# Expert retrieval of a streaming encoder layer: routing of a tile begins in the last third of the tile in front of its own, and selection is dealt out over 29 fours instead of 21

## The reference, cut to what matters

```python
q = (xb @ w_query).reshape(PEER_BLOCK, PEER_HEADS, 2, D_HALF)      # 8 heads, 2 halves, 128
s = einsum('thpd,hpkd->thpk', q, sub_keys)                         # 128 keys a half
sv, si = lax.top_k(s, 16)                                          # 16 lists of scores
cand = sv[:, :, 0, :, None] + sv[:, :, 1, None, :]                 # 256 sums a head
fv, fi = lax.top_k(cand.reshape(..., 256), 16)
eidx = take_along_axis(cidx, fi);  g = softmax(fv)
a = einsum('thkd,td->thk', expert_u[eidx], xb)
w = g * gelu(a)
out = einsum('thk,thkd->td', w, expert_v[eidx])
```

## Time and profile before

| | before |
|---|---|
| median of 3 runs | 3683.89 us (3681.74 to 3687.78) |
| the profiled execution's own time | 3686.14 us |
| its span, first to last instruction | 3684.3 us |
| busy TensorE, VectorE, ScalarE, GpSimd | 86%, 63%, 20%, 30% of the span |
| granted TensorE clock, mean over the span | 0.985 |
| bytes read from HBM | 1260.12 MB |

### The profile page before, as it was taken

How to read it: one execution, slowest core, us unless ns; L and a number is a source line. 1 busy time by engine, 2 the same in 40 slices (tenths; PEclk the granted TensorE clock), 3 DMA queues, 4 the chain that set the end, 5 groups by cost and what they waited for, 6 DMA issues and landing times.

```text
span 3684.3 us, 48012 instructions
## 1 busy us (share of the span) xinstructions
PE 3158.2 (86%) x17895; PEld 1389.9 (38%) x17895; DVE 2311.1 (63%) x6107; ACT 719.1 (20%) x2373; POOL 1110.6 (30%) x1177
## 2 busy tenths in 40 slices
PE   6999999889888878988887898889788888977776
PEld 3545556634334324423432343344234334422222
DVE  1333343867757866775776677677667757765444
ACT  2434434311111111111111111111111111111111
POOL 0000000033333333333333333333333333333332
PEclk8999999799999999999999999999999999999999
DMA  5000114299999999999999999999999999999997
GB/s 217 24 29 23 35 34 169 91 401 421 421 421 419 418 414 417 413 414 420 415 414 420 416 414 415 417 418 416 412 417 416 416 416 418 413 414 420 419 418 326
DMA packets 192682, 1275.60 MB, mean 346 GB/s; under 512 B 21056, under 2 KB 24768, under 8 KB 44608
## 3 DMA queue, kind: packets, MB, share of 16 engines
q0 software_dynamic: 165888, 1208.03, 79.4%
q1 hardware_dynamic: 26560, 64.49, 4.9%
HBM read 1260.12 MB, written 12.32 MB: 345 GB/s over the span
## 4 chain that ended last, share of the span: by engine, by line
DMA 46%; PE 35%; DVE 9%; issue 5%; POOL 4%; ACT 1%; SPq 0%; DVEq 0%; POOLq 0%; ACTq 0%
DMA arena<-in_experts,arena 45%; PE PS L1353 10%; PE PS L1182 8%; PE PS L1367 7%; POOL arena L651 4%; DVE arena L976 4%; PE PS L1276 3%; PE PS L1166 2%; PE PS L1399 2%; PE PS L1265 1%; PE PS L1225 1%; DVE arena L1051 1%; DVE arena L1054 1%; DVE arena L1057 1%; PE PS L1205 0%
## 5 line engine op out<-in xcount | busy, mean ns | idle before, releaser
L1353 PE MATMUL PS<-arena 128*128 128x512 bf16 x6912 | 1655.6, 382 | 453.1 <-DVE arena L976 440.6
L976 DVE CUSTOM_DVE_ANT_0 arena<-arena,PS 128x1024 f32<-128x1024 f32 x1152 | 1396.2, 1221 | 871.7 <-DMA arena<-in_experts,arena 548.4
L651 POOL DMA_INDIRECT arena<-in_experts,arena x1152 | 1089.0, 945 | 1938.0 <-PE PS L1367 1572.7
L1353 PEld LDWEIGHTS PS<-arena 128*128 128x128 bf16 x6912 | 611.5, 98 | 1480.5 <-DVE arena L976 865.1
L1367 PE MATMUL PS<-arena 128*32 128x512 f32 x4608 | 558.8, 603 | 16.8 <-ACT arena L867 16.8
L861 ACT ACTIVATE arena<-arena 128x4 f32<-128x4 f32 x288 | 59.5, 207 | 2156.2 <-DVE arena L976 2137.0
L1182 PE MATMUL PS<-arena 128*128 128x512 f32 (+1 forms) x720 | 309.8, 567 | 13.9 <-DMA arena<-in_w_in 7.9
L1399 PEld LDWEIGHTS PS<-arena 128*128 128x128 f32 x2304 | 266.6, 192 | 101.5 <-issue 101.5
L1399 PE MATMUL PS<-arena 128*128 128x128 f32 x2304 | 289.7, 280 | 0.0
L867 ACT ACTIVATE arena<-arena 128x1 f32<-128x1 f32 x1152 | 245.5, 284 | 9.4
L1367 PEld LDWEIGHTS PS<-arena 128*32 128x32 f32 x4608 | 120.8, 109 | 313.9 <-issue 175.4
(11 more groups left out here) (124 smaller groups left out, 1526.8 us busy)
## 6 DMA issues: line engine op xcount, KB each, us to landing
arena<-in_experts,arena POOLq DMA_INDIRECT x1152
arena<-in_w_in SPq DMA_DIRECT2D x8, 1024.0 KB, 11.8
arena<-in_w_query SPq DMA_DIRECT2D x4, 2048.0 KB, 16.1
arena<-in_xT SPq DMA_DIRECT2D x9, 512.0 KB, 3.9
h_scratch<-arena SPq DMA_DIRECT2D x9, 512.0 KB, 2.9
arena<-h_scratch SPq DMA_DIRECT2D x9, 512.0 KB, 8.1
out<-arena SPq DMA_DIRECT2D x9, 512.0 KB
arena<-in_x_prompt SPq DMA_DIRECT2D x8, 512.0 KB, 3.5
```

What stands on the lines that cost most here:

```text
L651: pool.indirect_dma_start(out=uv[r], out_offset=None, in_=experts, in_offset=bass.IndirectOffsetOnAxis(ap=expert_T[t % 2][:, tok:tok + 1], ...
L976: dve.tensor_tensor_reduce(uv[r][:, 0:D], uv[r][:, 0:D], xb(n), 1.0, 0.0, ALU.mult, ALU.add, a_dot[(n // 4) % 2][:, n % 4:n % 4 + 1]).then ...
L1353: mm = pe.matmul(PS[:, 2 + 2 * (n % 2) + c, :], pick[:, tok:tok + 1].broadcast_to([P, P]), parts[t % 2][k][:, 512 * c:512 * c + 512], star ...
```

## The change: what it does

The three tables are now keyed by the number of the four in the whole loop, and `schedule` puts in the steps of one tile. For the routings of tiles 1 and 2 the places stay as they were. For tiles 3 to 8 (six routings, which lie in the loop's tiles 1 to 7) they move, in fours counted from the start of the tile in front of the routed one:

| step | before | after |
|---|---|---|
| `norm` / `x2T` | -3 / -2 | -13 / -11 |
| `q` | -1 to 17, 4 of 5 fours | -10 to -7, -2 to 1, 4 to 7, 11 to 14 |
| `keys` | 3, 8, 13, 18 | -4, 2, 8, 15 |
| selection | 4 to 24 | -3 to 24 |
| `shift`, `gates` | 24, 25 | 25, 26 |
| transposes, `turned` | 26, 27 | 27, 28 |

So while the end of one selection runs in a tile, the norm, the transpose and the first queries of the next routing are already done in it. For that, the expert numbers are transposed into a free part of the keys' PSUM bank instead of the queries' bank, the rest of the split goes into `x2` itself instead of a scratch buffer that selection uses, and some waits follow.

```diff
+def schedule(t, norm, x2T, q_at, select, select_fours, last):
+    zero = (t - 1) * FOURS
...
+        if i % 4 == 3:
+            wait = 2 if t > 2 and i == 3 else 0
+            at(ACT_AT, zero + four + 1, t, "q", i // 4)
+            at(PE_AT, zero + four + 1 + wait, t, "keys", i // 4)
+            at(ACT_AT, zero + four + 2 + wait, t, "keys", i // 4)
...
+        at(DVE_AT, zero + select + spent * select_fours // length, t, *s)
...
+schedule(2, -3, -2, [-1] + [f for f in range(19) if f % 5 != 3], 4, 21, 24)
+for t in range(3, NT):
+    schedule(t, -13, -11, [four + l for four in (-10, -2, 4, 11) for l in range(4)], -3, 29, 25)
...
-                        ch.mark(dve.tensor_tensor(left, x2, parts[p][0], ALU.subtract))
+                        dve.wait_ge(x2T_psum, t + 1)
+                        ch.mark(dve.tensor_tensor(x2, x2, parts[p][0], ALU.subtract))
...
                     if step == "turned":
                         dve.wait_ge(turn_psum, 2 * t + 1)
-                        dve.tensor_copy(expert_T[p], PS[:, Q_FIRST if t == 0 else Q_BANK, 0:P]).then_inc(routed, 1)
+                        if t:
+                            dve.wait_ge(gate_T_ready, t + 1)
+                        dve.tensor_copy(expert_T[p], PS[:, K_BANK, P:2 * P] if t else PS[:, Q_FIRST, 0:P]).then_inc(routed, 1)
...
                         if k:
                             pe.wait_ge(key_ready, 4 * t + k)
+                        elif t >= 3:
+                            pe.wait_ge(routed, t)
+                            pe.wait_ge(gate_T_ready, t)
```

More of the change, by code:

```diff
@@ L63, with at @@
     SELECTION += [("sums", k), ("best", k, 0), ("experts", k, 0), ("best", k, 1), ("experts", k, 1)]
[L69 to L72, removed]
+PE_AT, ACT_AT, DVE_AT = {}, {}, {}
+def at(table, four, t, *step):
+    table.setdefault(four, []).append((t, *step))
+def schedule(t, norm, x2T, q_at, select, select_fours, last):
+    zero = (t - 1) * FOURS
+    at(ACT_AT, zero + norm, t, "norm")
+    at(DVE_AT, zero + norm, t, "norm")
+    at(PE_AT, zero + x2T, t, "x2T")
+    at(ACT_AT, zero + x2T + 1, t, "x2T")
+    high, low = (1, 1) if t == 1 else (0, 1)
+    at(DVE_AT, zero + high, t, "split_high")
+    at(DVE_AT, zero + low, t, "split_low")
+    for i, four in enumerate(q_at):
+        at(PE_AT, zero + four, t, "q", i // 4, i % 4)
@@ L87, in schedule @@
[L87 to L98, removed]
@@ L100 @@
-PE_EARLY = {30: [("x2T",)], 31: [("q", 0, 0)]}
-ACT_EARLY = {29: [("norm",)], 31: [("x2T",)]}
-DVE_EARLY = {29: [("norm",)]}
+    at(DVE_AT, zero + last, t, "shift")
+    at(ACT_AT, zero + last + 1, t, "gates")
+    at(DVE_AT, zero + last + 1, t, "gates")
+    at(PE_AT, zero + last + 2, t, "turn_experts")
+    at(PE_AT, zero + last + 2, t, "turn_gates")
+    at(ACT_AT, zero + last + 3, t, "turned")
+    at(DVE_AT, zero + last + 3, t, "turned")
+schedule(1, 0, 1, [2 + 5 * (i // 4) + i % 4 // 2 for i in range(16)], 5, 21, 25)
@@ L411, in build @@
         expert_of = shared[:, (TOPK + H) * CAND:].rearrange("p (a b) -> p a b", b=CAND)
-        left = shared[:, 0:D]
         sv = carve(16, TOPK)
@@ L850, in _ @@
                     for f in range(FOURS):
[L851 to L856, removed]
+                        n = t * FOURS + f
+                        for step in ACT_AT.get(n, ()):
+                            route(*step)
                         if t and f == SQUARES_AT:
                             squares(t - 1)
-                        n = t * FOURS + f
                         act.wait_ge(dots_ready, 4 * n + 4)
@@ L1152, in _ @@
                                 finish(t - 1)
-                        if t + 1 < NT:
-                            for step, *k in DVE_AT[t == 0].get(f, ()):
-                                route(t + 1, step, *k)
-                        if t + 2 < NT:
-                            for step, *k in DVE_EARLY.get(f, ()):
-                                route(t + 2, step, *k)
+                        for step in DVE_AT.get(n, ()):
+                            route(*step)
                 collect(NT - 1)
@@ L1484, in _ @@
                         weigh_experts(n, 1)
-                        if t + 1 < NT:
-                            for step, *k in PE_AT[t == 0].get(f, ()):
-                                route(t + 1, step, *k)
-                        if t + 2 < NT:
-                            for step, *k in PE_EARLY.get(f, ()):
-                                route(t + 2, step, *k)
+                        for step in PE_AT.get(n, ()):
+                            route(*step)
 def kernel(x_prompt, x_sample, cache_a_k, cache_a_v, cache_b_k, cache_b_v, norm1_g, w_in, rel_bias, sinks,
```

20 lines of the change are left out of this document (6 added, 14 removed).

## The result

| | before | after |
|---|---|---|
| median | 3684.22 us (3680.68 to 3687.86, 14 runs) | 3690.20 us (3687.85 to 3693.80, 14 runs) |
| ratio to before, 95% interval | | 1.0017 (1.0010 to 1.0024) |
| span of the profiled execution | 3684.3 us | 3687.5 us |
| mean granted TensorE clock | 0.985 | 0.984 |

I had expected 3683 with a range of 3673 to 3691. The median lies at the range's upper end, and the interval of the ratio excludes both no change and any gain. A loss of 0.17% was inside what I had called "within 0.2%"; 14 runs of each tell it from zero all the same.

What follows compares the result with a forecast made beforehand. The prediction took the gathers on the DMA queue to bound the loop. Its terms, -3.2 + 2.2 + 0 = -1.0 us, took the profiled 3686.14 us to 3685.1 and gave a median of 3683, range 3673 to 3691.

Steps and rivals of the forecast that it cites:

- within 0.2%: Outcome class for the whole kernel: a change of under 7.4 us either way, given a chance of 0.69.
- The split in place: Work term, VectorE's split written into `x2`: as many elements read and written as before, 0 us.
- Full fours: Selection stretches: fours in which VectorE has no slack drop from seven to five, a gain of 3.2 us.
- The ceiling of 14.9 us: Six selection stretches of tiles 2 to 7: the most any routing arrangement could gain by raising them to 420 GB/s.
- Selection in fours that had none: Fours 29 to 31 and 0 to 3 now hold selection and slow the gathers: 2.2 us lost, middle of 0 and 4.3.
- TensorE: Projections move to fours 22 to 25; the clock falls at four 24 move and do not vanish: 0 us.
- the 0.9 us for each: Price of one fall of TensorE's clock at four 24, from 399 against 418 GB/s over 20 us.
- The other waits: Moved or new waits at `turned`, the gates' transpose, `keys` and `norm`, all expected to be covered: 0 us.
- The port: Rival: two VectorE operations a tile each hold back a gather issue by 0.7 us, 8.4 us, giving 3691; chance 0.04.
- Thinner load: Rival: selection spread thinner frees the gathers, all of it 16.5 us, giving 3667; chance 0.20 for over 7.4 us.
- a wait as the bound: Rival: `routed` over 15.9 us late stalls each tile, at 5 us a tile 3713; chance 0.01.
- the signs: If right: selection stretches 416 to 418 GB/s, tile starts 416 or 417, four to eight lowered-clock stretches, VectorE's data wait changed under a tenth.

Runs made afterwards that it cites:

- e2: The kernel before with only the in-place split and its wait for the transpose x2T: 3690.65 us, ratio to before 1.0018.
- e4: e1 with the selection of tiles 3 to 8 left out, tile 2's expert numbers used again: 3671.13 us, ratio to before 0.9962.
- e9: e1 with only the `experts` steps of tiles 3 to 8 left out: 3683.41 us, ratio to before 0.9998.
- e12: e4 with 272 one-column copies a tile added on VectorE, each with its semaphore increment: 3682.68 us, ratio to before 0.9996.
- e14: e4 with 48 long two-input operations of 128x800 a tile added on VectorE: 3671.80 us, ratio to before 0.9965.
- e17: e4 with 136 one-column copies a tile added on VectorE, half as many as e12: 3677.36 us, ratio to before 0.9979.
- e1: The changed kernel, but tile 1's split writes to scratch as before and has no wait: 3684.91 us, ratio to before 1.0002.
- e7: e1 with eight projection matmuls repeated behind fours 16, 17, 19 and 20 of tiles 2 to 7: 3683.56 us, ratio to before 0.9999.
- e11: e1 with tile 1's routing one four later (3680.56 us) plus e7's repeated matmuls: 3680.47 us.

## Why the prediction was wrong

- **The step that failed** is in the waits, and in the sentence on work: "The split in place reads and writes as many elements as before: 0." It priced the elements and passed over the wait on `x2T_psum` that stands in the diff with it. Of the waits I went through `turned`'s, `keys`' and `norm`'s, and not this one; and I read the change in the middle of the loop, where the transpose is ten fours ahead, not in tile 0, whose routing was said to be unchanged in its places. The places were; the wait was new. Measured: 4.51 us of VectorE idle, and 6.9 us of time for the split and its wait alone (e2), where the sum had 0 for both.
- **Full fours, -3.2.** The ceiling of 14.9 us was right in size (e4: 13.8), and what it hung on was wrong. It does not go with full fours: with four of the five gone, e9 gains 1.5 us. It goes with VectorE's number of instructions (e12, e14, e17), which the change leaves as it is.
- **Selection in fours that had none, +2.2.** Its sign is seen: 3005 to 3065 us fell from 421 to 415, and the starts of tiles 2 to 6 from 419.0 to 417.4 in the mean. If each instruction has its price, it is the gain of the selection stretches given back (415.0 to 415.7 in the mean of the six), so that both terms are one and sum to 0. That is argued and not shown; my -1.0 for the two lies inside e1's interval, and the runs can't tell it from 0.
- **TensorE, 0.** Right as a sum: falls moved from four 24 to four 18. Their number was too high, two in tiles 1 to 7 for the four to eight I had expected, and the 0.9 us for each was not found (e7, e11, e14).
- **The other waits, 0.** Right: behind tile 0 no time stands at `routed` or at the gates' transpose, and e1, which has all of them but the split's in tile 0, can't be told from the kernel before.
- **The port.** Both of its overlaps are seen, and each is smaller than the rival's price. In the timeline after, the gather issue at four 19 of tile 3 begins inside `norm`'s last operation.

```profile
1930.63 1.28 DVE L1000 SCALAR_TENSOR_TENSOR arena<-arena 128x1024 f32<-128x1024 f32 x1
...
1931.66 1.06 POOL L656 DMA_INDIRECT arena<-in_experts,arena  x1 [3.63 <-PE PS L1367]
```

  It takes 1.06 us instead of 0.94, 0.12 longer for an overlap of 0.25; so it is in five of the six tiles. The first issue behind four 1 begins inside the second product of `experts` in all six: in tile 3, at 1747.54 us, it takes 1.14 us, 0.20 longer for an overlap of 0.32. Together these eleven make 1.8 us of issue and not 8.4, and e1, which has eleven such issues too, shows no loss that can be told. The 3691 that this rival gave is near the measured 3690 by chance only.
- **Thinner load** (3667) and **a wait as the bound** (3713) did not come. The second had the right kind, a new wait, in the wrong place and as a price for each tile; it was one wait in one tile.

Of the signs, stretches at 415 and 416 fell just short of the 416 to 418 named, those at a tile's start lie between 414 and 420 and not at 416 or 417, two falls came for four to eight, and VectorE's wait for data grew by 13% where I had said less than a tenth.

## What to carry to other kernels

List every wait that a diff adds, and for each every place where it runs, the first pass of the loop above all: there the producer may stand right beside the consumer, while in the steady state it is long done. An edit "in place" swaps a buffer for an order, and the order has a price. In a loop bound by its gathers, before spreading work more evenly, find out by leaving it out and by putting dummy work in its place which of its measures (busy time, number of instructions, fullest slot) the loss goes with; here it went with the number of VectorE's instructions, which spreading them leaves as it is.

## What the runs showed of the hardware that was not expected

- 1787 VectorE instructions beside the gathers cost 13.8 us of DMA time, some 7.7 ns each: 1597 copies of one column cost 11.6 us, 280 operations of 0.99 us 0.7. What joins the count to the gathers is open. The same copies on ScalarE cost nothing (1733 of them: -1.2 us). DMA still shows as busy throughout, at 416 instead of 418 or 419 GB/s.
- An idle gap of 4.51 us on VectorE cost 6 us of time in tile 0 (6.9 in e2), more than its own length: GpSimd's next gathers went out 5.5 us later, and two and a half fours of gathers in flight did not cover it. The granted clock of the stretch fell to 0.91 as well; the runs don't separate the two.
- A fall to 1.2 GHz that lengthens 24 matmuls from 5.67 to 7.24 us cost nothing that 11 runs can tell, although the 20 us around it moved 393 GB/s instead of 418 in one case (411 in the other).
- A gather issue that begins inside a VectorE operation with two inputs in SBUF is lengthened, but by less than the overlap: 0.12 us for 0.25, 0.20 for 0.32, and 0.70 for 0.82.
